# A decoder step in which value gathers, rotary key copies, gating tiles, a weight load and a square are placed anew

## The chip, the cores and the metric

The kernel runs on one core of a Trainium2 chip. The metric is the time of one execution in microseconds (us), less is better. Three timed runs of the kernel before gave 1568.81, 1569.15 and 1570.91 us, so the median is 1569.15 us.

## The reference, cut to what matters

Two layers of a hybrid decoder run for 512 prompt tokens and for 8 x 4 sample tokens (544 columns in all), in float32, with 1024 channels. Layer 0 has one input projection, a short gated convolution and a latent attention; layer 1 has a spatial gating unit. Each layer ends in a squared-ReLU MLP and a gated embedding.

```
a = rms(h);  hc, gc, gb, cq, ckv, kpe = split(a @ w_in)
kpe = rope(kpe);  q_lat = q_nope @ w_uk            # layer 0
prompt: s = q_nope.(ckv w_uk) + q_pe.kpe, causal softmax, @ (ckv w_uv)
sample: s = q_lat.past_c + q_pe.past_p over 16 pages of 128 cached rows each,
        softmax, @ past_c, then @ w_uv              # pages picked by page_table
z = gelu(a @ w_in_c);  u, v = z[:, :1024], rms(z[:, 1024:])   # layer 1
s = tril(w_s[g]) @ v[chunk, g] + b_s;  h += (u * s) @ w_out_c # g = 0..7
y = rms(h) at the very end
```

## The kernel before, in words

Activations lie with channels on the partitions, as eight chunks of 128 x 544. Weights come in 99 units of 1 MB through a ring of four slots; SyncE (SP) issues their loads in order. Each engine's list of instructions is written out by hand and the engines meet at semaphores.

The places that matter here, in order of time:

- **Start.** SP issues the loads of the gains, of the first quarter of the input, of weight unit 0, of the other three quarters, and so on. ScalarE copies each chunk times its gain into `A` (L892, semaphore `x_ready`), then squares the chunks (L896). TensorE's `in_ab(0)` and `in_ab(1)` (L480) read unit 0: 64 matmul records, chunk by chunk.
- **Key fetch.** `keys(m)` in the SP block fetches eight pages of the cached keys (144 KB each) into `kring`, whose four slots hold two such groups. From m = 2 on it waits until TensorE has scored group m - 2 (`k_scored`). `score_pair(m)` (L617) reads group m.
- **Value gathers.** POOL gathers the cached rows for the value product with indirect DMAs, four for each of 16 steps s, 1 MB a step (L423). The list `V_ORDER` gives the order 0..7, 10..13, 8, 9, 14, 15. Steps 0, 1, 6, 7, 8, 9, 14 and 15 use two buffers in the arena; the others lie in the four ring slots. Each gather of s >= 6 waits until TensorE has used an earlier buffer (`v_used`). `values_pair` (L652) reads step s.
- **Between projection and attention.** DVE ends the last convolution and the running maximum (`raw_max`, `soft_max`), copies the rotary rows of the keys from `ssum` to the eight heads of `K` (L1339, eight copies of 32 x 512), and then copies the other 64 rows of each head from PSUM (L1342, L1343), which releases the PSUM tiles `T_UK`. TensorE computes these tiles (L680) and the value tiles (L688), with the transposes of the sample probabilities (L639) between them. ScalarE exponentiates the sample scores (L914, `soft`).
- **Attention loop.** It has 32 prompt items n = 0..31 (L722 scores, L731 transposes, L743 values). `paged(n)` puts the sample work between them: `values_pair(0, n/2)` at even n below 16, `score_pair(8 + n//2)` at odd n below 16, and `values_pair(1, n - 24)` from n = 24 to 31. So key group m = 10 is needed at n = 5, 11 at 7, 12 at 9, 13 at 11, 14 at 13, 15 at 15, and step 8 + r is needed at n = 24 + r.
- **Gating.** The gMLP projection is done as groups of seven products (P1, P3, P2, P6, P5, P7, P4; L510). The dictionary `SPATIAL` says after which product of which later group a small tile is computed, all in two PSUM banks in turn: `n0` (L772) the norm of v, `t0`..`t7` (L777) transposes of one group, `T0`, `T1` (L780) transposes of the sample tokens, `M0` (L789) their mixing by 32-column matmuls, `m0`..`m7` (L784) the mixing of group g. The key ("u", j, k) stands for group j + 4 and the product k, counted 0 to 6. A tile waits until the tile two before it has been read, `M0` until `T1` has, and `m` g until `t` g has. DVE reads the tiles in the same order (L1440, L1434, L1443, L1449), but all those behind the products 0, 1 and 2 only when it has read P2, in one block (`hook(0, 1, 2)` of `combine`). POOL forms products of the gates (L450) and sums (L438 to L441).
- **End.** In `gates(1)` ScalarE takes, for each of the last eight chunks of h, first the copy times the gain (`norm_chunk`, L821) and then the square (L827), which DVE adds up (L1008) for the last norm.

## Time and profile before

| what | value |
|---|---|
| median of 3 timed runs | 1569.15 us |
| the profiled execution | 1552.78 us |
| its span, first to last instruction | 1551.0 us |
| TensorE busy | 1490.4 us, 96% |
| VectorE (DVE) busy | 1004.4 us, 65% |
| ScalarE busy | 253.8 us, 16% |
| mean granted TensorE clock | 0.981 |

The profiled execution is one run with the profiler on; it is 16.4 us shorter than the median of the timed runs. The span lies 1.8 us below its time. All stretches below are in microseconds from the start of the span. A PEclk of 1.00 is 2.4 GHz, 0.50 is 1.2 GHz. A wait row reads: who waited, for whom, total, number of times, the longest.

### The profile page before, as it was taken

The numbers are of one execution on the slowest core, as the hardware profiler recorded it, in microseconds if no ns is written. First come the engines' busy times: TensorE is split into PE (matmuls) and PEld (weight loads), VectorE is DVE, ScalarE is ACT, GpSimd is POOL, SyncE is SP. The second block draws the span as 40 slices with busy tenths as digits, with TensorE's granted clock in tenths as the row PEclk, the third lists the DMA queues.
The fourth block names the chain that finished last, engine by engine and source line by source line (L and its number), as shares of the span: only waits on it lengthen the run. The fifth ranks groups of instructions, "written<-read, shape, count | busy, mean of one in ns | idle before, by whom it ended". The sixth has DMA issues, their size and how long they took to land.

```text
span 1551.0 us, 18751 instructions
## 1 busy us (share of the span) xinstructions
PE 1490.4 (96%) x7096; PEld 1199.1 (77%) x7096; DVE 1004.4 (65%) x2020; ACT 253.8 (16%) x527; POOL 80.9 (5%) x90
## 2 busy tenths in 40 slices
PE   7999978899999999999999998999999999999995
PEld 6887734578888888888888777788888888888884
DVE  3363364868776776766755776877866767767644
ACT  4000022512101101001222320021001011011222
POOL 0012224200000000000000001300000000000000
PEclk9999998999999999999999999999999999999997
DMA  8305669422222222222213111222222222222101
GB/s 326 109 22 163 197 174 281 159 74 85 75 85 86 82 87 83 82 82 91 86 55 113 63 74 55 62 84 78 84 84 85 84 87 82 86 85 97 66 19 58
DMA packets 39323, 152.35 MB, mean 98 GB/s; under 512 B 6657, under 2 KB 19362, under 8 KB 26434
## 3 DMA queue, kind: packets, MB, share of 16 engines
q1 hardware_dynamic: 34114, 134.37, 25.0%
q0 software_dynamic: 5120, 16.78, 3.6%
q8 instruction: 57, 0.93, 0.2%
q14 instruction: 32, 0.26, 0.1%
HBM read 148.11 MB, written 3.02 MB: 97 GB/s over the span
## 4 chain that ended last, share of the span: by engine, by line
PE 92%; DVE 4%; DMA 2%; issue 1%; SPq 1%; ACT 0%; DVEq 0%
PE psum L510 66%; PE psum L480 20%; DMA arena<-in_keys 1%; PE psum L617 1%; PE psum L465 1%; PE psum L722 1%; SPq L361 1%; PE psum L743 0%; PE psum L688 0%; PE psum L602 0%; DMA ring<-in_weights 0%; PE psum L652 0%; PE psum L784 0%; DVE small L1361 0%; DVE A L1498 0%
## 5 line engine op out<-in xcount | busy, mean ns | idle before, releaser
L510 PE MATMUL psum<-arena 128*128 128x272 f32 x1920 | 457.4, 395 | 0.0
L510 PEld LDWEIGHTS psum<-arena 128*128 128x128 f32 x1920 | 366.7, 191 | 75.0
L1049 DVE TENSOR_TENSOR arena<-psum,arena 128x272 f32<-128x272 f32 x544 | 240.0, 441 | 247.6 <-PE psum L510 226.0
L480 PE MATMUL psum<-A,ring 128*128 128x272 f32 x832 | 196.8, 399 | 7.8 <-DMA ring<-in_weights 7.8
L480 PEld LDWEIGHTS psum<-A,ring 128*128 128x128 f32 x832 | 160.2, 193 | 43.2 <-DMA ring<-in_weights 7.8
L510 PE MATMUL psum<-B,ring 128*128 128x272 f32 x704 | 177.9, 396 | 4.0 <-issue 3.7
L510 PE MATMUL psum<-arena,ring 128*128 128x272 f32 x640 | 159.7, 393 | 0.0
L510 PEld LDWEIGHTS psum<-B,ring 128*128 128x128 f32 x704 | 134.1, 191 | 32.1 <-issue 4.4
L510 PE MATMUL psum<-A,ring 128*128 128x272 f32 x576 | 144.4, 393 | 1.5 <-DVE A L1423 1.5
L510 PEld LDWEIGHTS psum<-arena,ring 128*128 128x128 f32 x640 | 121.5, 190 | 24.6
L510 PEld LDWEIGHTS psum<-A,ring 128*128 128x128 f32 x576 | 109.5, 190 | 24.4 <-DVE A L1423 2.0
L844 ACT ACTIVATE arena<-psum 128x272 f32<-128x272 f32 x80 | 31.7, 396 | 541.9 <-PE psum L510 541.9
L510 PE MATMUL psum<-B,arena 128*128 128x272 f32 x352 | 88.3, 393 | 0.0
L510 PEld LDWEIGHTS psum<-B,arena 128*128 128x128 f32 x352 | 67.0, 191 | 13.6
L510 PE MATMUL psum<-A,arena 128*128 128x272 f32 x288 | 72.2, 393 | 0.0
L1029 DVE TENSOR_TENSOR arena<-ring 128x512 f32<-128x512 f32 x80 | 55.5, 694 | 13.1 <-DVE arena L1043 9.6
L1193 DVE TENSOR_TENSOR arena<-psum,rstd 128x544 f32<-128x544 f32 x18 | 12.9, 724 | 78.2 <-PE psum L480 78.0
L510 PEld LDWEIGHTS psum<-A,arena 128*128 128x128 f32 x288 | 54.8, 190 | 11.2
L1109 DVE TENSOR_TENSOR h<-h,arena 128x272 f32<-128x272 f32 x128 | 56.5, 442 | 4.4
L1108 DVE TENSOR_TENSOR arena<-arena,rstd 128x272 f32<-128x272 f32 x128 | 56.5, 441 | 4.4
L480 PE MATMUL psum<-B,ring 128*128 128x272 f32 x256 | 58.8, 393 | 0.0
L1032 DVE TENSOR_TENSOR arena<-ring 128x512 f32<-128x512 f32 x80 | 56.3, 703 | 2.8
(200 smaller groups left out, 1270.0 us busy)
## 6 DMA issues: line engine op xcount, KB each, us to landing
ring<-in_weights SPq DMA_DIRECT2D x99, 1024.0 KB, 4.8
arena<-in_keys SPq DMA_DIRECT2D x128, 144.0 KB, 5.0
arena<-in_attw SPq DMA_DIRECT2D x1, 3072.0 KB, 21.0
h<-in_xT SPq DMA_DIRECT2D x4, 544.0 KB, 7.4
out_yT<-A SPq DMA_DIRECT2D x8, 272.0 KB, 2.3
arena<-in_pemb SPq DMA_DIRECT2D x2, 544.0 KB, 5.8
arena<-in_bias SPq DMA_DIRECT2D x1, 640.0 KB, 6.3
B<-in_rope SPq DMA_DIRECT2D x1, 544.0 KB, 12.6
```

The source lines that it names most:

```text
L361: sp.dma_start(kring[:, s % 4, i % 4, :, :].rearrange("p c n -> p (c n)"), a["keys"][bass.ds(pages[i], 1), :, :].rearrange("o p n -> (o p) ...
L465: last = pe.matmul(slot(t)[:, i, 0:TH], ones[:], c[:, TH * i:TH * i + TH], start=n == 0, stop=n == len(chunks) - 1)
L480: last = pe.matmul(slot(t)[0:w.shape[-1], i, 0:TH], w, x[:, k, TH * i:TH * i + TH], start=k == 0, stop=k == ks - 1)
L510: end = pe.matmul(bank(g, n), lhs[:, c, :], x(c), start=c == 0, stop=c == 3)
L617: last = pe.matmul(psum[32 * bb:32 * bb + 32, 4, 256 * (m % 2):256 * (m % 2) + 256], qx[:, c, P * g + 32 * bb:P * g + 32 * bb + 32], kring ...
L722: pe.matmul(psum[:, n % 2, 0:(i + 1) * P], Q[0:96, hd, i * P:(i + 1) * P], K[0:96, hd, 0:(i + 1) * P], start=True, stop=True).then_inc(sc_ ...
L844: act.activation(p1_of(g), bank(g, P1), ACT.Copy).then_inc(p1_read, 1)
L1029: link(dve.tensor_tensor(wsum(g, 1), quarter(u, 1, 0), quarter(u, 1, 1), ALU.add))
L1032: dve.tensor_tensor(wsum(g, 3), quarter(u, 0, 0), quarter(u, 1, 0), ALU.subtract)
L1049: ins = dve.tensor_tensor(out, bank(g, n), more, ALU.add)
L1108: link(dve.tensor_tensor(x, x, rstd[:, half], ALU.mult))
L1109: link(dve.tensor_tensor(h[:, m, half], h[:, m, half], x, ALU.add))
```

## The change

Six edits: `V_ORDER` is dropped, so the gathers go 0 to 15; each keeps a wait on `v_used`, and steps 10 to 13 also wait until prompt items 16, 18, 20 and 22 have been scored (`sc_full` 17, 19, 21, 23). The eight copies of rotary key rows go from DVE to ScalarE, behind its fourth raw copy and ahead of its exponentials; TensorE waits for them (`k_rope`) before the first item. `SPATIAL` moves T0, t2, T1, m2, m3, t6 and t7. Weight unit 0 is loaded in two halves, the second after the second quarter of the input, and TensorE waits for each half on its own. In the last norm ScalarE squares a chunk before it copies it.

```diff
-SPATIAL = {("u", 0, 3): ["n0"], ("u", 0, 5): ["t0"], ("u", 0, 6): ["t1"],
-           ("u", 1, 0): ["T0"], ("u", 1, 1): ["t2"], ("u", 1, 2): ["T1"], ...
-           ("u", 2, 0): ["t4"], ("u", 2, 1): ["t5"], ("u", 2, 2): ["m2"], ...
+SPATIAL = {("u", 0, 3): ["n0"], ("u", 0, 4): ["T0"], ("u", 0, 5): ["t0"], ("u", 0, 6): ["t1"],
+           ("u", 1, 0): ["t2"], ("u", 1, 1): ["T1"], ("u", 1, 3): ["M0"], ...
...
-V_ORDER = [0, 1, 2, 3, 4, 5, 6, 7, 10, 11, 12, 13, 8, 9, 14, 15]
...
                 if i == 0:
-                    unit(0)
+                    sp.dma_start(ring[:, 0, 0:UNIT // 2], a["weights"][0][:, 0:UNIT // 2]).then_inc(w_first, 16)
+                elif i == 1:
+                    sp.dma_start(ring[:, 0, UNIT // 2:], a["weights"][0][:, UNIT // 2:]).then_inc(w_loaded[0], 16)
...
-            for n, s in enumerate(V_ORDER):
+            for s in range(16):
                 if 2 <= s < 6:
                     pool.wait_ge(psum_full, T_COL[2 * (s + 3) + 1] + 1)
                 elif s >= 6:
-                    pool.wait_ge(v_used, n - 5)
+                    pool.wait_ge(v_used, {6: 1, 7: 2, 8: 7, 9: 8, 14: 9, 15: 10}.get(s, s - 7))
+                if 10 <= s < 14:
+                    pool.wait_ge(sc_full, 2 * s - 3)
...
+                    if n == 0 and k == 0:
+                        pe.wait_ge(w_first, 16)
+                    elif n == 0 and k == 4 or n and n % 2 == 0 and k == 0:
+                        pe.wait_ge(w_loaded[u % SLOTS], 16 * (u // SLOTS + 1))
...
             pe.wait_ge(psum_free, T_OUTAB)
+            pe.wait_ge(k_rope, H)
...
+                if n == 6:
+                    square_chunk(n, m)
                 act.activation(X[:, m, :], h[:, m, :], ACT.Copy, scale=gain(n, m)).then_inc(x_ready, 1)
-                square_chunk(n, m)
+                if n != 6:
+                    square_chunk(n, m)
...
                 raw(0, r)
+            act.wait_ge(ql_ready, 2)
+            act.wait_ge(psum_full, T_COL[17] + 1)
+            for hd in range(H):
+                act.activation(K[64:96, hd, :], ssum[64:96, 0:TP], ACT.Copy).then_inc(k_rope, 1)
...
             soft_max(0)
-            for hd in range(H):
-                link(dve.tensor_copy(K[64:96, hd, :], ssum[64:96, 0:TP]))
```

The value gathers on POOL, from step 6 on, before:

```order
L423 DMA arena<-in_rows,vidx 128x512 [waits v_used]
L423 DMA arena<-in_rows,vidx 128x512 x3
L423 DMA arena<-in_rows,vidx 128x512 [waits v_used]
L423 DMA arena<-in_rows,vidx 128x512 x3
L423 DMA ring<-in_rows,vidx 128x512 [waits v_used]
L423 DMA ring<-in_rows,vidx 128x512 x3
```

And from step 6 on in the changed kernel:

```order
L426 DMA arena<-in_rows,vidx 128x512 [waits v_used]
L426 DMA arena<-in_rows,vidx 128x512 x3
L426 DMA arena<-in_rows,vidx 128x512 [waits v_used]
L426 DMA arena<-in_rows,vidx 128x512 x3
L426 DMA arena<-in_rows,vidx 128x512 [waits v_used]
L426 DMA arena<-in_rows,vidx 128x512 x3
L426 DMA arena<-in_rows,vidx 128x512 [waits v_used]
L426 DMA arena<-in_rows,vidx 128x512 x3
L426 DMA ring<-in_rows,vidx 128x512 [waits sc_full,v_used]
L426 DMA ring<-in_rows,vidx 128x512 x3
```

Steps 6 and 7 stay first, but the ring steps 10 to 13 now stand behind steps 8 and 9 and have a second wait.

TensorE in gating group ("u", 1, ...), from P3 to M0 (L510 is P3, P2 and P6, L777 is t2, L780 is T1, L789 is M0), before:

```order
L510 MATMUL psum<-B,arena 128x272 [waits dve_read,wsum_ready]
L510 MATMUL psum<-B,arena 128x272 x3
L777 MATMUL psum<-ident,arena 128x128 [waits psum_free]
L777 MATMUL psum<-ident,arena 128x128 x3
L510 MATMUL psum<-B,ring 128x272 [waits dve_read]
L510 MATMUL psum<-B,ring 128x272 x3
L780 MATMUL psum<-ident,arena 32x128 [waits psum_free]
L780 MATMUL psum<-ident,arena 32x128 x3
L510 MATMUL psum<-arena 128x272 [waits xt_ready,dve_read]
L510 MATMUL psum<-arena 128x272 [waits xt_ready] x3
L789 MATMUL psum<-arena 128x32 [waits psum_free]
L789 MATMUL psum<-arena 128x32 x7
```

The same products in the changed kernel (L513 is P3, P2 and P6; L790 is T1; L799 is M0):

```order
L513 MATMUL psum<-B,arena 128x272 [waits dve_read,wsum_ready]
L513 MATMUL psum<-B,arena 128x272 x3
L790 MATMUL psum<-ident,arena 32x128 [waits psum_free]
L790 MATMUL psum<-ident,arena 32x128 x3
L513 MATMUL psum<-B,ring 128x272 [waits dve_read]
L513 MATMUL psum<-B,ring 128x272 x3
L513 MATMUL psum<-arena 128x272 [waits xt_ready,dve_read]
L513 MATMUL psum<-arena 128x272 [waits xt_ready] x3
L799 MATMUL psum<-arena 128x32 [waits psum_free]
L799 MATMUL psum<-arena 128x32 x7
```

T1 now stands ahead of P2, and nothing stands between P2 and P6; M0 keeps its place behind P6.

## Rows read from the trace of the kernel before

**Rows 1.** The page, part 1: busy us, share of the span, instructions.

```profile
PE 1490.4 (96%) x7096; PEld 1199.1 (77%) x7096; DVE 1004.4 (65%) x2020; ACT 253.8 (16%) x527; POOL 80.9 (5%) x90
```

**Rows 2.** Waits of TensorE: who, for whom, total us, times, longest.

```profile
PE psum L617 <- DMA arena<-in_keys: 10.6, 4, 4.2
PE psum L480 <- DMA ring<-in_weights: 7.8, 1, 7.8
```

**Rows 3.** Timeline of the start: start us, us, instruction [idle before <-releaser].

```profile
6.59 1.39 ACT L892 ACTIVATE A<-h,gains 128x544 f32<-128x544 f32 x2
7.76 16.72 PE L480 MATMUL psum<-A,ring 128*128 128x272 f32 x64 [7.76 <-DMA ring<-in_weights]
```

**Rows 4.** Chain of waits, whole span: start us, us, what.

```profile
25.40 36.67 PE psum L480 x160
```

**Rows 5.** Timeline between projection and attention, three engines.

```profile
191.31 1.28 ACT L914 ACT_TABLE_LOAD   x1
196.92 0.72 ACT L914 ACTIVATE arena<-arena,small 128x512 f32<-128x512 f32 x1 [4.33 <-DVEq L1226]
...
196.98 3.59 DVE L1339 COPY A<-ssum 32x512 f32<-32x512 f32 x8
...
202.12 3.39 PE L680 MATMUL psum<-arena 128*128 128x512 f32 x4 [4.69 <-DVEq L1344]
...
206.07 1.88 PE L688 MATMUL psum<-arena 128*128 128x512 f32 x4
...
215.29 0.49 PE L722 MATMUL psum<-A,arena 96*128 96x128 f32 x2 [0.67 <-DVE arena L1348]
```

**Rows 6.** Timeline of TensorE in the attention loop, scores of cached keys.

```profile
217.12 1.50 PE L617 MATMUL psum<-arena 96*32 96x256 f32 x24
...
230.24 2.79 PE L617 MATMUL psum<-arena 96*32 96x256 f32 x24 [4.10 <-DMA arena<-in_keys]
...
255.63 2.79 PE L617 MATMUL psum<-arena 96*32 96x256 f32 x24 [4.19 <-DMA arena<-in_keys]
```

**Rows 7.** Stretches: length, busy us of PE, PEld, DVE, ACT, POOL, PEclk, DMA, GB/s.

```profile
219.00:270.00 51.00, 40.41 (x367) 20.29 (x366) 21.73 (x74) 15.14 (x42) 25.72 (x28) 0.83 1.03 282
...
255.60:264.00 8.40, 8.37 (x50) 3.72 (x51) 2.32 (x7) 1.65 (x4) 0.88 (x2) 0.50 1.06 301
...
272.00:293.00 21.00, 17.81 (x144) 11.48 (x139) 17.82 (x64) 13.06 (x40) 1.65 (x2) 1.00 0.13 39
```

**Rows 8.** DMA issues up to 40 us: issues, KB, median us to landing.

```profile
arena<-in_keys SPq DMA_DIRECT2D x16, 144.0 KB, 2.5
```

**Rows 9.** Timeline of POOL: first gathers of steps 10 and 14.

```profile
227.08 0.95 POOL L423 DMA_INDIRECT ring<-in_rows,vidx  x1 [0.30 <-issue]
...
293.23 0.94 POOL L423 DMA_INDIRECT arena<-in_rows,vidx  x1 [19.27 <-PE psum L652]
```

**Rows 10.** Timeline of DVE before and during the gathers of step 14.

```profile
292.85 0.43 DVE L1040 TENSOR_TENSOR arena<-B 128x272 f32<-128x272 f32 x1
...
296.52 0.44 DVE L1041 TENSOR_TENSOR arena<-B,arena 128x272 f32<-128x272 f32 x1
```

**Rows 11.** Timeline of DVE and TensorE in the gating tiles.

```profile
941.03 0.74 DVE L1440 TENSOR_SCALAR arena<-psum,arena 32x512 f32<-32x512 f32 x1
...
941.82 0.61 PE L780 MATMUL psum<-ident,arena 128*32 128x128 f32 x4 [1.99 <-DVE arena L1440]
...
944.20 1.97 PE L789 MATMUL psum<-arena 32*128 32x32 f32 x16
...
962.41 1.16 PE L784 MATMUL psum<-arena 128*128 128x128 f32 x8 [1.95 <-DVE arena L1434]
963.41 3.52 PE L510 MATMUL psum<-arena 128*128 128x272 f32 x8
```

**Rows 12.** Stretch behind 3.8 us of 32-column matmuls (L602), same columns as 7.

```profile
107.00:113.00 6.00, 6.00 (x25) 4.86 (x25) 2.39 (x9) 0.00 (x0) 1.45 (x2) 0.50 0.01 3
```

**Rows 13.** Timeline of ScalarE at the end.

```profile
1533.52 0.75 ACT L821 ACTIVATE A<-h,gains 128x544 f32<-128x544 f32 x1 [1.55 <-DVE h L1174]
```

More of the change, by code:

```diff
@@ L52 @@
 T_SP = T_N3 + 1
-SPATIAL = {("u", 0, 3): ["n0"], ("u", 0, 5): ["t0"], ("u", 0, 6): ["t1"],
[4 rows of a table removed]
+SPATIAL = {("u", 0, 3): ["n0"], ("u", 0, 4): ["T0"], ("u", 0, 5): ["t0"], ("u", 0, 6): ["t1"],
+           ("u", 1, 0): ["t2"], ("u", 1, 1): ["T1"], ("u", 1, 3): ["M0"], ("u", 1, 4): ["m0"], ("u", 1, 5): ["m1"],
+           ("u", 1, 6): ["t3"],
+           ("u", 2, 0): ["t4"], ("u", 2, 1): ["t5"], ("u", 2, 3): ["m2"], ("u", 2, 4): ["m3"], ("u", 2, 5): ["t6"],
+           ("u", 2, 6): ["t7"],
            ("u", 3, 0): ["m4"], ("u", 3, 1): ["m5"], ("u", 3, 3): ["m6"], ("u", 3, 5): ["m7"]}
@@ L251, in build @@
         x_loaded = [sem(f"x_loaded{i}") for i in range(4)]
+        w_first = sem("w_first")
         gains_loaded = sem("gains_loaded")
@@ L284, in build @@
         ql_ready = sem("ql_ready")
+        k_rope = sem("k_rope")
         qs_ready = sem("qs_ready")
@@ L572, in in_ab, with lhs @@
                 u = n // 2
-                if n % 2 == 0:
-                    pe.wait_ge(w_loaded[u % SLOTS], 16 * (u // SLOTS + 1))
                 w = ring[:, u % SLOTS, :].rearrange("p (k m) -> p k m", k=KD)
-                tile(T_COL[n], lambda k: w[:, k, (n % 2) * P:(n % 2 + 1) * P], A, KD, x_ready, 0)
+                def lhs(k):
+                    if n == 0 and k == 0:
+                        pe.wait_ge(w_first, 16)
+                    elif n == 0 and k == 4 or n and n % 2 == 0 and k == 0:
+                        pe.wait_ge(w_loaded[u % SLOTS], 16 * (u // SLOTS + 1))
+                    return w[:, k, (n % 2) * P:(n % 2 + 1) * P]
+                tile(T_COL[n], lhs, A, KD, x_ready, 0)
             in_ab(0)
```

4 rows, old and new, of the table SPATIAL are left out of this document.

## The prediction

> **What bounds the kernel now.** I read the page's busy times first: TensorE is busy for 1490.4 of 1551.0 us [rows 1], so a gain can only come from TensorE's idle time and from stretches in which it runs at half its clock. The list of TensorE's waits then says where it idles: 10.6 us for cached keys, four times, and 7.8 us for the first weights [rows 2]. The timelines place the other waits: 4.69 us for DVE ahead of the fourth key tile [rows 5], 1.99 and 1.95 us in the gating tiles [rows 11]. Last I read stretches for the granted clock and the DMA share, because after a long wait the work also costs more: the same 24 records of key scores take 1.50 us at full clock and 2.79 us behind a wait of 4.1 or 4.2 us [rows 6]. Each edit aims at one of these places, and they lie apart in time, with TensorE continuously busy between them, so the savings add.
>
> **Rotary copies to ScalarE.** DVE loses eight copies, 3.59 us [rows 5], between its maximum and its copies from PSUM. TensorE waits there: its last key tile (202.12) needs DVE's first two PSUM copies, which now start at 196.98 instead of 200.60. So it starts 3.6 us earlier, at 198.5. Its wait shrinks from 4.69 to about 1.1 us. In the row the four matmuls took 3.39 us; the same shape takes 1.88, of which some 0.15 overlaps the next, when the clock is up [rows 5], so about 1.7 us more are saved, and 0.3 on the transposes behind them, if 1.1 us of idle time leaves the clock alone. What is late next: DVE has 6.2 us of PSUM copies to do, until 203.2, then four pairs of 1.4 us for the value tiles; TensorE needs 2.2 us a pair and stays the slower one, so the first item moves from 215.29 to about 209.7. ScalarE is free at 191.31 and idle for 4.33 us before its exponential [rows 5]. A copy of 128 x 544 takes 0.70 us there [rows 3]; a 32 x 512 copy on ScalarE is not in the trace: between 0.45 (DVE's own, 3.59 / 8) and 0.70 us. I take 0.65: eight end at 196.5, the table load of 1.28 us follows, and the first exponential ends near 198.6, ahead of the transpose that needs it at 200.2. At 0.70 us it is still ahead; the cover would be gone at about 0.9. Gain 5.6 us, at least 3.6 (clock stays low) and at most 5.9.
>
> **Gathers.** From 219 to 270 us the DMA engines are full and move 282 GB/s [rows 7], that is 14.4 MB: the key groups 10 to 15 at 1.18 MB each and seven or eight value steps at 1.05 MB. Uncontended, a key fetch lands 2.5 us after its issue [rows 8], and the eight issues of a group take 4.0 us, so a group needs 6.5 us from its release. The loop gives 7.5 us for group 10 (release 218.62, when group 8 has been scored, need 230.24 - 4.10 = 226.14 [rows 6]) and about 8.5 for each later one. With the gathers beside it a group gets less than half of the bandwidth and is late. The edit takes steps 10 to 13 (4.2 MB, 14.9 us at 282 GB/s) out of this stretch into 264 to 284, where the DMA share is 0.13 [rows 7].
>
> - Group 10: its wait (4.10 us) is over at 230.24; step 10 starts only at 227.08 [rows 9], behind steps 6 and 7 in POOL's queue, which stay. I let this wait and its slow clock stand.
> - Groups 11, 12 and 13: the other 10.6 - 4.1 = 6.5 us of waits. By 235 all of groups 10, 11 and steps 6, 7 (4.5 MB) has landed, and 11 is needed at 239. Group 13 is needed at 249.1 (255.63 - 4.19 [rows 6] less the 2.3 of the two smaller waits); it is released 8.5 us before that, at 240.6, and lands by 247.5. So 6.5 us go.
> - The clock: 255.6 to 264.0 runs at 0.50 with TensorE busy for 8.37 us [rows 7]. Without the wait before it, about 4.0 us go (half of 8.37 less small waits for other engines).
> - Steps 8 and 9 now come a little earlier relative to group 15, which has 9 us for 6.5 us of transfer plus a share; I leave 0.
>
> POOL needs 5.0 us for a step (four issues 1.25 apart). From item 12 it now has eight steps in a row, 40 us, ending 19 items and 46 us later. Step 15 starts about 1.0 us later relative to its use: last issue 7.2 us ahead of need, 8.3 before. I charge 0.1 us, at most 1. Gain 10.4 us; from 2.3 (only small waits go) to 17.6 (also group 10 with its clock, 4.1 + 3.1).
>
> The trace says that gathers do not disturb DVE: a tensor_tensor of 272 columns takes 0.43 us before and 0.44 during the gathers of step 14 [rows 10], and DVE is busy for 17.8 of 21 us where they go now [rows 7]. The Trainium skill (GPSIMD Engine Reference, Specifications) says that POOL's SBUF interfaces are shared with VectorE and contend with instructions that have two SBUF inputs; by that rule these operations would be slowed; the row speaks against it for DMA issues, and the rival below on this has a small chance.
>
> The Trainium skill (DMA: Bandwidth & Descriptors, Queues, rings and completion order) says each DMA engine goes round its queues packet by packet. The trace agrees: group 10 lands 11.6 us after its release in place of 6.5. By the rule group 10, still beside steps 6 and 7, stays late, and the sum is the one below.
>
> **First unit in halves.** TensorE starts at 7.76, when 1 MB has landed; the first chunk from ScalarE is ready at 7.28 (6.59 + half of 1.39) [rows 3]. Half the weights come before that. So it starts 0.45 us earlier. The 64 records took 16.72 us; at the later pace (36.67 / 160 = 0.229 each) [rows 4] they would take 14.7, so 2 us are lost to a slow start that the edit does not touch. The later input quarters arrive as before. Gain 0.45, from 0 to 0.6.
>
> **Square ahead of its copy.** The last chunk's square waits behind its copy of 0.75 us [rows 13], of which 0.66 precedes the square's start. The chain runs square, DVE sum, ones tile, root, reciprocal, products. The copy is needed only 8 us later. Gain 0.66, from 0.6 to 0.75.
>
> **Gating tiles.** Work on TensorE is the same. Two waits change.
>
> - T1 waited 1.99 us for DVE's read of T0, which stood behind P2 [rows 11]. Now T0 is read a group earlier. But M0 stands behind P6 (1.83 us) and needs DVE to finish P2's read and scaling (1.2 us), t2 (0.95: 1.95 - 1.2 for its main part, as at t4, and some 0.2 for its sample columns) and T1 (0.74) [rows 11], so 2.9 us: a new wait of 1.06 us.
> - m2 waited 1.95 us for t4. Behind P6 that shrinks to 0.1. And P6, 3.52 us at half clock behind that wait [rows 11], gets back about 1.7, its neighbours 0.2.
> - Does the clock fall at M0? Its 1.97 us of 32-column matmuls [rows 11] now follow 1.06 us of idle time. Such thin matmuls do let it fall: behind 3.8 us of them it is 0.50 [rows 12]. A wait of 1.99 us did not; 1.95 us and then 1.16 us of 128-column matmuls did [rows 11]. That case, 3.1 us in all, is nearest to 3.0 here, so I charge 1.7 us. At the other end it is 0.
> - POOL's sums now start behind t7, one product later, and overlap two-input DVE work of the next group: 0.2 us.
>
> So 0.9 + 3.8 - 1.7 - 0.1 = 2.9 us, from 0.5 to 4.7.
>
> **Sum.** 5.6 + 10.4 + 0.45 + 0.66 + 2.9 = 20.0 us, from 1552.78 to 1532.8 for a profiled execution. The timed runs lie 16.4 us higher; I take the same difference off their median: 1569.15 - 20.0 = 1549.1 us.
>
> **Rivals.**
>
> - *Keys are late for their own sake.* With only two groups in the ring, the release and not the bandwidth would bind. For: 7.5 us against 6.5 is close, and group 10 is still late and shifts the others. Against: full DMA share throughout [rows 7]. Then a long wait and its slow clock stay, 8.2 us: 1557.3.
> - *The first wait goes too.* If steps 6 and 7 leave group 10 more room than I think, 7.2 us more: 1542.
> - *A new gating wait eats the gain.* DVE gets t2 and T1 in one block, and the clock falls for longer: 1552.
> - *POOL's issues slow DVE.* If operations with two SBUF inputs, about a quarter of DVE's 17.8 us in 272 to 293 [rows 7], doubled while POOL issues, 4.5 us would be lost: 1553.6. Rows 10 speak against it.
> - *Slower: the gathers come too late.* POOL delivers a step in 5.0 us, but items 24 to 31 use one in 2.4. If steps 10 to 15 were not ahead by item 24, they would take 6 x 5.0 + 6 us of landing against 18 us of items, 18 us more, and the clock would fall in each of six waits, about 1 us each: 1549 + 24 = 1573. It decides only when step 10 is issued 15 us later than the 264 us that I work out, which would need item 16 or step 9 to be that late. Nothing shows that.
> - *Several sizes fail at once.* The clock stays low in the rotary stretch, keys stay late, gating gives 0.5: 1562.
>
> **How the numbers follow.** Forecast 0.58, gating 0.08, slowed DVE 0.02, late keys 0.15, first wait gone 0.08, several at once 0.05, gathers late 0.04. The forecast's own range is 1546 to 1552. Late keys (1557) belong inside the 8 in 10, and half of the better case: 1543 to 1558. A measurement here can tell 0.2%, 3.1 us, from no change. Faster by more than that 0.93, within it 0.03 (several at once, with worse sizes), slower 0.04.
>
> **What would show it.** In the changed profile: TensorE's first record near 7.3; the first item near 209 to 210 and the last key tile at about 1.7 us; waits for cached keys down from 10.6 us to about 4, once, with the clock at 0.50 for one stretch of 6 us and not for the second; DMA busy between 264 and 284; no wait of TensorE on values from item 24; no wait ahead of m2's P6, one of about 1 us at M0; the last DVE sum 0.66 us nearer to the last projection record. A key wait of 4 us around group 12 or 13, or a PE wait at L652's counterpart, would prove me wrong.

## The result and the profile after

The changed kernel takes 1557.62 us (median of six runs, 1553.16 to 1559.05). The kernel before took 1568.62 us beside it (six runs). The ratio is 0.9928, 95% interval 0.9910 to 0.9946, so about 11 us are gained. The forecast was 20.0 us and 1549.1 us. The direction held and the gain is little over half of what was forecast. The time lies 0.4 us inside the wider range (1543 to 1558) and outside the forecast's own (1546 to 1552). Below, a gain against the kernel before is the ratio's share of its time. The profiled execution took 1554.70 us, with a span of 1552.7.

The page of the changed kernel, part 1, against [rows 1]: TensorE has about as much to do, and ends no earlier than in the profile of before. Part 4 of the page (the chain that ended last) names a source that the page of before does not have.

```profile
PE 1494.4 (96%) x7096; PEld 1199.0 (77%) x7096; DVE 1002.3 (65%) x2012; ACT 258.1 (17%) x535; POOL 81.6 (5%) x90
...
PE 92%; DVE 4%; another core or an unknown queue 2%; issue 1%; ACT 1%; DMA 0%; DVEq 0%; SPq 0%; ACTq 0%
```

The start and the end, TensorE, against [rows 3] and the last rows of the chain. Columns: start us, length us, instruction, and the idle time before it with what ended it.

```profile
7.36 16.79 PE L483 MATMUL psum<-A,ring 128*128 128x272 f32 x64 [7.36 <-ACT A L905]
...
1537.35 2.18 PE L468 MATMUL psum<-ssum,ones 128*128 128x272 f32 x4 [4.47 <-DVE ssum L1025]
```

TensorE now starts on ScalarE's first chunk and no longer on weights. The next group of the chain starts at 25.07 and not at 25.40 [rows 4]: 0.33 us. At the end, TensorE's ones matmuls wait 4.47 us for the last sum, where the same four waited 5.11 before: 0.64 us.

The rotary stretch (ScalarE, then TensorE), against [rows 5]:

```profile
193.78 0.60 ACT L922 ACTIVATE arena<-psum 128x512 f32<-128x512 f32 x1 [13.07 <-remote]
194.40 4.25 ACT L952 ACTIVATE A<-ssum 32x512 f32<-32x512 f32 x8
198.67 1.28 ACT L927 ACT_TABLE_LOAD   x1
```

```profile
187.51 2.80 PE L626 MATMUL psum<-arena 96*32 96x256 f32 x48
194.43 1.49 PE L635 MATMUL psum<-arena 96*128 96x32 f32 x6 [4.12 <-ACT arena L922]
195.73 8.67 PE L689 MATMUL psum<-arena 128*128 128x512 f32 x16
```

The eight copies cost ScalarE 0.53 us each, and the 4.69 us wait at the fourth key tile is gone: L689 runs its 16 matmuls in one piece. But there is a new wait of 4.12 us ahead of them. ScalarE's copy of the scores could start when L626 ended at 190.3. It starts 3.5 us later, and the profile can name no source for that ("remote": another core or an unknown queue).

Such waits return in the attention loop. Waits from 185 to 330 us, columns: who for whom, us in total, times, longest:

```profile
ACT arena L922 <- remote: 18.4, 3, 13.1
ACT arena L971 <- remote: 17.8, 6, 6.5
PE psum L741 <- DVE rbuf L1384: 15.0, 7, 3.8
DVE psum L1373 <- remote: 10.6, 5, 3.8
DVE arena L1249 <- remote: 4.0, 1, 4.0
POOL arena L426 <- remote: 1.5, 1, 1.5
```

Cached keys are no longer in this list [rows 2]. In their place TensorE waits 15.0 us for DVE, which itself stood still. One such place in the timeline:

```profile
255.21 0.66 PE L753 MATMUL psum<-arena 128*64 128x128 f32 x8
255.26 0.19 ACT L961 ACTIVATION_READ_ACCUMULATOR rbuf<-psum,small 128x1 f32 x1
255.70 0.94 POOL L426 DMA_INDIRECT arena<-in_rows,vidx  x1 [0.30 <-issue]
255.80 1.12 PE L732 MATMUL psum<-A,arena 96*128 96x512 f32 x2
256.76 0.49 PE L741 MATMUL psum<-ident,rbuf 128*128 128x128 f32 x3
256.94 0.95 POOL L426 DMA_INDIRECT arena<-in_rows,vidx  x1 [0.30 <-issue]
...
259.03 0.30 DVE L1373 TENSOR_TENSOR psum<-psum,masks 128x128 f32<-128x128 f32 x1 [3.76 <-remote]
259.08 0.49 ACT L971 ACTIVATE arena<-psum 128x384 f32<-128x384 f32 x1 [3.63 <-remote]
...
260.83 0.55 PE L741 MATMUL psum<-ident,rbuf 128*128 128x128 f32 x3 [1.52 <-DVE rbuf L1384]
```

DVE's add needs the scores of L732, ready at 256.9; ScalarE's copy needs the transposes of L741, ready at 257.3. Both start at 259.0 to 259.1, together, 1.1 us after GpSimd's fourth issue.

The trace also holds the time of every semaphore update, which these views don't print. At this place (us):

```
TensorE's work            record ends   update    later by
L626 scores, cached keys  255.28        258.87    3.59
L753 values of an item    255.87        258.96    3.09
L732 scores of an item    256.93        259.01    2.08
L661 values, cached rows  258.26        259.22    0.96
```

DVE and ScalarE start 0.02 us after the update they wait for. From 185 to 330 us, 21 of 64 updates by TensorE come more than 0.5 us after the end of the matmul record that makes them; in the profile of before all of 137 come within 0.05 us. (Counted are semaphores of which every update is on record.) So the unnamed waits are waits for TensorE whose signal is recorded late; the instructions of DVE and ScalarE are not late themselves.

The clock falls behind TensorE's own wait in several such places. Stretches (columns as in [rows 7]):

```profile
268.00:272.00 4.00, 3.66 (x23) 2.93 (x24) 2.47 (x13) 2.05 (x6) 2.26 (x3) 0.50 0.78 197
288.00:292.00 4.00, 3.42 (x21) 2.53 (x19) 2.24 (x8) 1.27 (x3) 2.28 (x3) 0.50 0.66 188
304.00:308.00 4.00, 3.54 (x22) 1.37 (x15) 2.17 (x8) 0.84 (x3) 0.32 (x1) 0.50 0.56 157
```

The gating tiles, TensorE, against [rows 11]:

```profile
944.38 0.60 PE L790 MATMUL psum<-ident,arena 128*32 128x128 f32 x4
...
949.78 1.94 PE L799 MATMUL psum<-arena 32*128 32x32 f32 x16 [1.14 <-DVE arena L1455]
951.65 2.10 PE L513 MATMUL psum<-arena 128*128 128x272 f32 x8
...
967.97 1.16 PE L794 MATMUL psum<-arena 128*128 128x128 f32 x8
968.97 2.00 PE L513 MATMUL psum<-arena 128*128 128x272 f32 x8
```

T1 (L790) and m2 (L794) no longer wait, M0 (L799) waits 1.14 us, and in this profile the product behind M0 and the one behind m2 run at full clock (2.10 and 2.00 us; behind m2 it was 3.52 before).

### The profile page after: what moved, and what is told of

The parts are those of the page before. It is cut to its first block, busy times and chain, and to the rows that moved or that the text cites. A ratio compares the mean times of both kernels' runs of the same rounds, so it can differ in the third digit from the quotient of the medians.

```text
span 1552.7 us, 18767 instructions
## 1 busy us (share of the span) xinstructions
PE 1494.4 (96%) x7096; PEld 1199.0 (77%) x7096; DVE 1002.3 (65%) x2012; ACT 258.1 (17%) x535; POOL 81.6 (5%) x90
## 3 DMA queue, kind: packets, MB, share of 16 engines
q1 hardware_dynamic: 34258, 134.37, 24.8%
## 4 chain that ended last, share of the span: by engine, by line
PE 92%; DVE 4%; another core or an unknown queue 2%; issue 1%; ACT 1%; DMA 0%; DVEq 0%; SPq 0%; ACTq 0%
PE psum L513 65%; PE psum L483 19%; PE psum L626 1%; PE psum L732 1%; PE psum L468 1%; PE psum L661 1%; PE psum L753 1%; PE psum L689 1%; DVE small L1376 1%; PE psum L697 0%; PE psum L741 0%; PE psum L611 0%; DVE rbuf L1384 0%; PE psum L794 0%
## 5 line engine op out<-in xcount | busy, mean ns | idle before, releaser
L513 PE MATMUL psum<-arena 128*128 128x272 f32 x1920 | 455.7, 393 | 0.0
L513 PEld LDWEIGHTS psum<-arena 128*128 128x128 f32 x1920 | 365.0, 190 | 75.0
L513 PE MATMUL psum<-B,ring 128*128 128x272 f32 x704 | 177.9, 395 | 4.1 <-issue 3.7
L513 PE MATMUL psum<-arena,ring 128*128 128x272 f32 x640 | 159.7, 392 | 0.0
L513 PEld LDWEIGHTS psum<-B,ring 128*128 128x128 f32 x704 | 133.9, 191 | 32.2 <-issue 4.4
L513 PE MATMUL psum<-A,ring 128*128 128x272 f32 x576 | 144.4, 393 | 1.5 <-DVE A L1438 1.5
L513 PEld LDWEIGHTS psum<-arena,ring 128*128 128x128 f32 x640 | 121.3, 190 | 24.8
L513 PEld LDWEIGHTS psum<-A,ring 128*128 128x128 f32 x576 | 109.3, 190 | 24.6 <-DVE A L1438 1.9
L513 PE MATMUL psum<-B,arena 128*128 128x272 f32 x352 | 88.3, 393 | 0.0
L513 PEld LDWEIGHTS psum<-B,arena 128*128 128x128 f32 x352 | 66.9, 191 | 13.7
L513 PE MATMUL psum<-A,arena 128*128 128x272 f32 x288 | 72.2, 392 | 0.0
L513 PEld LDWEIGHTS psum<-A,arena 128*128 128x128 f32 x288 | 54.7, 190 | 11.3
```

Of the source, the lines that this page charges most:

```text
L513: end = pe.matmul(bank(g, n), lhs[:, c, :], x(c), start=c == 0, stop=c == 3)
```

## The experiments

Each set of runs shared one chip and its own runs of the kernel before. The results give that chip the number 0 in sets 1 and 3 and 15 in set 2; whether both 0 are the same piece isn't on record. In the first set the kernel before took 1554.03 us, in the second 1566.08, in the third 1564.87, beside the changed kernel's result 1568.62. That the kernel before differs by 11 to 15 us from one to the other turned out to be half of the explanation. The table gives the stretches of the attention loop from the profile of each kernel, from the starts of items 0, 6 and 16 and of the output projection (L513's first record), in us:

```
kernel               unnamed waits   item 0-6   6-16    16-out   sum      ratio
before               no              18.71      38.49   47.38    104.58
set 1  before again  no              18.00      38.38   47.40    103.78   1.0005
       gathers only  no              19.45      29.34   50.60     99.39   0.9951
       all but them  no              19.95      37.28   46.60    103.83   0.9933
       rotary only   no              18.65      38.20   46.57    103.42   0.9959
result changed       yes             19.87      29.75   62.86    112.48   0.9928
set 2  changed again yes             20.62      31.18   61.43    113.23   0.9927
       gating only   yes             20.14      43.82   55.00    118.96   0.9976
       6, 7 later    yes             13.26      36.47   62.77    112.50   0.9926
       10 early      yes             15.67      42.06   71.53    129.26   1.0030
set 3  rows left out no              12.70      26.76   47.72     87.18   0.9781
       rows straight no              20.37      30.71   47.77     98.85   0.9850
       spread        yes             13.41      41.37   61.35    116.13   0.9970
       changed, 3rd  yes             19.70      29.68   62.61    111.99   0.9936
```

("Unnamed waits" are those after item 0. Every kernel of sets 2 and 3 has the one at 190 us.)

**The kernel before once more** (`e1_before_again`, no edit):

> The kernel before, once more, timed against itself. Theory (the profiled execution of before was an unusually fast one: 1552.78 us, while six timed ones lay at 1565 to 1571, and the profile of the changed kernel shows waits of 3 to 4 us of ScalarE and VectorE on semaphores of an unknown source that the profile of before does not have): this run's profile has a span of 1563 to 1569 us and such waits in the stretch from 180 to 320 us. Rival (the waits are a product of the changed kernel): a span of about 1551 us and no such wait. The ratio of times should be 1.000 within 0.002 either way.

1553.81 us, ratio 1.0005 (0.9981 to 1.0028), and no such wait, as the rival had it. In this set the kernel before doesn't have them. Whether the changed kernel makes them, or something that differs from set to set, stayed open here.

**The gathers alone.** The gather order and the waits of the change, nothing else:

```
-            for n, s in enumerate(V_ORDER):
+            for s in range(16):
...
-                    pool.wait_ge(v_used, n - 5)
+                    pool.wait_ge(v_used, {6: 1, 7: 2, 8: 7, 9: 8, 14: 9, 15: 10}.get(s, s - 7))
+                if 10 <= s < 14:
+                    pool.wait_ge(sc_full, 2 * s - 3)
```

> Only the gathers' new order and their waits on prompt items are put into the kernel before. If the forecast's term holds: 10.4 us faster, ratio 0.9934. If late keys are bound by their two-group ring: 2 us, 0.9985. If the unknown waits come with the gathers, wherever these are: between, 4 to 8 us, and the waits of TensorE for keys go while waits on semaphores of unknown source stand at the gathers' new places from 255 us on.

1546.96 us, ratio 0.9951 (0.9925 to 0.9976), 7.6 us less. TensorE's timeline:

```profile
232.41 2.79 PE L619 MATMUL psum<-arena 96*32 96x256 f32 x24 [4.82 <-DMA arena<-in_keys]
...
305.65 1.15 PE L654 MATMUL psum<-arena 128*32 128x256 f32 x16 [2.10 <-DMA arena<-in_rows,vidx]
```

The last gather on GpSimd, and SyncE's queue issuing the four 1 MB weight units of the output projection:

```profile
296.43 0.95 POOL L425 DMA_INDIRECT arena<-in_rows,vidx  x1 [0.30 <-issue]
```

```profile
290.81 8.77 SPq L332 DMA_DIRECT2D ring<-in_weights  x4
```

One key wait is left, that of group 10, as forecast; items 6 to 16 gain 38.38 - 29.34 = 9.0 us. The wait of group 10, 4.82 us, lies among those of the four profiles with the old order and no unnamed waits (3.37, 4.04, 4.10 and 5.30). The rows of the last step come late: 2.10 us of waiting, 3.2 us from item 16 on. In the two profiles 4.4 us remain of the gain. The timed gain, 7.6 us, has an interval of 3.7 to 11.7, so it alone doesn't exclude the 10.4 of the forecast. It fits the third expectation in size only: there is no unnamed wait.

**All but the gathers.** The changed kernel with the gathers as before:

```
+V_ORDER = [0, 1, 2, 3, 4, 5, 6, 7, 10, 11, 12, 13, 8, 9, 14, 15]
...
-            for s in range(16):
+            for n, s in enumerate(V_ORDER):
...
-                    pool.wait_ge(v_used, {6: 1, 7: 2, 8: 7, 9: 8, 14: 9, 15: 10}.get(s, s - 7))
-                if 10 <= s < 14:
-                    pool.wait_ge(sc_full, 2 * s - 3)
+                    pool.wait_ge(v_used, n - 5)
```

> The changed kernel with the gathers' old order and waits. By the forecast's terms 9.6 us faster than before, ratio 0.9939 (rotary 5.6, start 0.45, square 0.66, gating 2.9). If the rotary copies on ScalarE start late (in the changed kernel's profile they began at 194.4, not 191.3, and gained 1.4 us up to the first prompt item): 5 to 6 us, 0.9965. With e2 the two should add up to the whole change, 0.9928, if the parts are independent.

1543.63 us, ratio 0.9933 (0.9914 to 0.9952), 10.4 us less; 9.6 were expected. The gating stage, from its first tile to the products that wait for its result (997.21 us before), took 69.21 us and 69.23 in the changed kernel, against 73.43 before: 4.2 us.

**The rotary copies alone.**

```
             pe.wait_ge(psum_free, T_OUTAB)
+            pe.wait_ge(k_rope, H)
...
             for r in range(4):
                 raw(0, r)
+            act.wait_ge(ql_ready, 2)
+            act.wait_ge(psum_full, T_COL[17] + 1)
+            for hd in range(H):
+                act.activation(K[64:96, hd, :], ssum[64:96, 0:TP], ACT.Copy).then_inc(k_rope, 1)
...
-            for hd in range(H):
-                link(dve.tensor_copy(K[64:96, hd, :], ssum[64:96, 0:TP]))
```

> Only the eight rotary copies go to ScalarE. By the forecast 5.6 us faster, ratio 0.9964, with the first prompt item 5.6 us earlier. If ScalarE's fourth raw copy waits for an unknown source for 3 us there as in the changed kernel's profile: about 1.5 to 2.5 us, 0.999.

1547.18 us, ratio 0.9959 (0.9940 to 0.9979), 6.4 us less, and no unnamed wait. From the scores of the cached keys ahead of it to item 0 took 22.19 us, against 27.30 in the run of before beside it: 5.1 us. TensorE's fourth key tile, against [rows 5]:

```profile
192.53 5.40 PE L681 MATMUL psum<-arena 128*128 128x512 f32 x12
199.00 1.98 PE L681 MATMUL psum<-arena 128*128 128x512 f32 x4 [1.08 <-DVEq L1348]
```

The wait is 1.08 us (forecast 1.1), the clock stays up (1.98 us and not 3.39).

**The changed kernel again** (`e7_after_again`, no edit):

> The changed kernel once more, nothing edited. Theory (the waits of DVE and ScalarE of which the profile names no source belong to that one chip or execution, and the parts add up): no such wait here, PE waits for the keys of group 10 alone as with the gathers only (about 4.8 us), from item 16 to the output projection about 50 us and not 62.9; the gathers gained 0.9951 and everything else 0.9933, so the ratio is 0.988 to 0.990 and the time 15 to 19 us under the kernel before. Rival (the waits come of the combination of the gathers with ScalarE's copies of the rotary keys): the waits of 3 to 4 us stand again between 190 and 303 us, and the ratio stays at 0.993.

1556.58 us, ratio 0.9927 (0.9901 to 0.9954), with the unnamed waits where they were. My rival had the ratio right. Its reason fell with the next kernel.

**The gating tiles alone.**

```
-           ("u", 1, 0): ["T0"], ("u", 1, 1): ["t2"], ("u", 1, 2): ["T1"], ("u", 1, 3): ["M0"], ("u", 1, 4): ["m0"],
+           ("u", 1, 0): ["t2"], ("u", 1, 1): ["T1"], ("u", 1, 3): ["M0"], ("u", 1, 4): ["m0"], ("u", 1, 5): ["m1"],
...
```

> The kernel before with the gating tiles dealt out anew, and nothing else. The prediction: 2.9 us gained, ratio 0.9981, with 1.7 us of it lost because the clock falls again at tile M0. The theory after the profile of the changed kernel (the clock doesn't fall at M0, and the stage took 69.2 us and not 73.4): 4.2 us gained, ratio 0.9973. Nothing changes before 900 us.

1563.45 us, ratio 0.9976 (0.9959 to 0.9992), 3.8 us less. The interval (1.3 to 6.4 us) holds both expectations. At M0 this profile shows what the prediction had charged for, a fall of the clock:

```profile
955.94 1.94 PE L789 MATMUL psum<-arena 32*128 32x32 f32 x16 [1.14 <-DVE arena L1440]
957.81 3.54 PE L510 MATMUL psum<-arena 128*128 128x272 f32 x8
```

The wait and the 32-column matmuls are those of the changed kernel's profile, where the same product took 2.10 us. Of the ten profiles with the new tiles, five show the fall (from this product to the tile behind it 2.56 to 3.53 us) and five don't (1.94 us each). In three of the five, this one among them, an earlier fall behind tile `n0`, which the others have, is missing, so that the stage is no longer for it: from `n0` to the product behind `m7` it takes 61.2 to 61.5 us in eight of the ten and 63.1 to 63.2 in the two that have both falls. With the old tiles four profiles show 64.3, 65.6, 65.8 and 69.3 us.

The weightier finding is elsewhere. This kernel is the kernel before up to 900 us, and it has the unnamed waits:

```profile
194.81 0.60 ACT L909 ACTIVATE arena<-psum 128x512 f32<-128x512 f32 x1 [13.00 <-remote]
227.52 0.60 ACT L909 ACTIVATE arena<-psum 128x512 f32<-128x512 f32 x1 [2.99 <-remote]
262.86 0.60 ACT L909 ACTIVATE arena<-psum 128x512 f32<-128x512 f32 x1 [3.89 <-remote]
310.78 0.28 ACT L954 ACTIVATE arena<-psum 128x128 f32<-128x128 f32 x1 [7.80 <-remote]
```

Its loop takes 118.96 us, the same code in set 1 103.78. That is 15.2 us of longer profile beside 12.0 us by which the kernel before is slower there (1566.08 - 1554.03). So the waits come neither from the new gather order nor from ScalarE's copies. The same program has them in one set and not in another. All profiles of sets 2 and 3 have at least the one at 190 us, and none of set 1 has any; what differs between the sets, the chip or something else, is not shown, and the number 0 stands on either side.

**Steps 6 and 7 later.** The changed kernel, and

```
+                if s == 6:
+                    pool.wait_ge(sc_full, 7)
```

> The changed kernel, with the gathers of steps 6 and 7 held back until the scores of item 6 are made, so that no gather is on the queues when the keys of group 10 land. Theory (the keys of group 10 land late because two steps of gathers share the queues with them): the wait for them falls from 4.8 us to about 2 (issued from 220.3 to 226.6 and 2.5 us to land, against PE that is ready at 227.5), the half clock behind it goes too (the score group 1.5 and not 2.8 us), together 3 to 5 us less than the changed kernel, ratio 0.985 to 0.988 against before. Rival (eight page transfers, each issued 0.8 us after the last, are late by themselves): the wait stays over 4 us and the time is that of the changed kernel.

1555.51 us, ratio 0.9926 (0.9899 to 0.9954). The key wait behaves as the theory says:

```profile
225.17 1.50 PE L628 MATMUL psum<-arena 96*32 96x256 f32 x24 [0.49 <-DMA arena<-in_keys]
```

0.49 us and full clock, and items 0 to 6 take 13.26 us and not 20.6. Group 10 is late because of steps 6 and 7 alone. But items 6 to 16 take 36.47 and not 31.2, because unnamed waits moved with the gathers: DVE stands for 2.96 us until 233.38 and ScalarE for 4.48 until 234.86, where they had none, and the pair that ended at 223.65 and 228.25 is gone. The time is the same, as the rival had it, and not the 3 to 5 us less of the theory. In a set without such waits this kernel was not run.

**Step 10 early.** The changed kernel, and

```
-            for s in range(16):
+            for s in [0, 1, 2, 3, 4, 5, 6, 7, 10, 8, 9, 11, 12, 13, 14, 15]:
...
-                if 10 <= s < 14:
-                    pool.wait_ge(sc_full, 2 * s - 3)
+                if s in (7, 10):
+                    pool.wait_ge(sc_full, 7)
```

> The changed kernel, with the gathers in the order 6, 7, 10, 8, 9, 11 to 15; steps 7 and 10 wait for the scores of item 6 and none of the later ones for scores at all, so that GpSimd's queue is one step (5 us) ahead when it comes to steps 14 and 15. Theory (steps 14 and 15 are late because GpSimd still issues steps 12 and 13 when their buffers come free): the wait of about 2 us for the rows at item 31 goes, and the stretch from item 31 to the output projection is 11 us again and not 14; with half of the gain at group 10 that is 4 to 6 us less than the changed kernel, ratio 0.984 to 0.987 against before. Rival (the gathers of steps 7 and 10 now meet the keys of groups 12 and 13, issued from about 235 to 250 us): a new wait of 2 to 4 us for those keys, and the time is that of the changed kernel or 2 us over it.

1571.16 us, ratio 1.0030 (1.0013 to 1.0047), 15 us over the changed kernel. Neither expectation held. GpSimd now issues sixteen gathers one behind the other, from 264.79 to 284.49, and in the second half of them DVE and ScalarE stand still:

```profile
275.32 0.78 PE L732 MATMUL psum<-A,arena 96*128 96x128 f32 x2
276.04 0.95 POOL L426 DMA_INDIRECT ring<-in_rows,vidx  x1 [0.30 <-issue]
...
283.54 0.95 POOL L426 DMA_INDIRECT ring<-in_rows,vidx  x1 [0.30 <-issue]
286.19 0.30 DVE L1373 TENSOR_TENSOR psum<-psum,masks 128x128 f32<-128x128 f32 x1 [11.50 <-remote]
...
287.58 0.60 ACT L971 ACTIVATE arena<-psum 128x512 f32<-128x512 f32 x1 [13.61 <-remote]
```

DVE resumes 1.7 us after the last gather of the burst was issued (283.54 + 0.95). The scores that it waits for have a record that ends at 271.64; their update comes at 286.10.

**The late gathers left out.** Steps 6 to 15 stay in HBM, TensorE multiplies old rows:

```
-            for s in range(16):
+            for s in range(6):
...
-                pe.wait_ge(v_loaded[v_slot(s)], 64 * (v_use(s) + 1))
+                pe.wait_ge(v_loaded[v_slot(s)], 64)
```

> The changed kernel without the gathers of steps 6 to 15: the rows stay in HBM, and TensorE multiplies what lies in the buffers (that part of the output is left out). It prices everything the late gathers cost, keys that come late and waits without a named source alike. Theory (both come of the gathers' transfers): after 226 us no wait without a named source on DVE, ScalarE or GpSimd, no wait for keys over 1 us, and from item 0 to the output projection 93 to 97 us, against 112.5 in the changed kernel where such waits stand and about 98 where they don't. Rival (the waits without a named source belong to the program or the chip whatever is transferred): DVE stands again for 3 to 4 us at its scores near 255 us and ScalarE near 285 us, and the stretch is over 105 us.

1530.18 us, ratio 0.9781 (0.9760 to 0.9803), 25.2 us under the changed kernel. No unnamed wait after item 0, no wait for keys among TensorE's, as the theory says, and the loop takes 87.18 us; I had expected 93 to 97. Late keys, late rows and stops together cost the changed kernel 24.8 us.

**The same bytes, in a line.** Steps 6 to 15 fetch 128 rows that lie together, from the same engine at the same points of the program (other rows than the table names):

```
+                    if s >= 6:
+                        k = 128 * ((4 * s + bb) % (rows.shape[0] // 128))
+                        pool.dma_start(v_buf(v_slot(s))[:, bb, :], rows[k:k + 128, :])\
+                            .then_inc(v_loaded[v_slot(s)], 16)
+                        continue
```

> The changed kernel, in which steps 6 to 15 fetch the same amount of bytes as 128 rows in a line and not as rows picked by an index (the rows are others than the table names, so the output is others'). Theory (it is the traffic, not the kind of transfer): keys late and waits without a named source are those of the changed kernel, to 2 us in the sum. Rival (it is what GpSimd does to write the descriptors of a gather): these waits go, and the stretch from item 0 to the output projection falls to 98 us or less, as with the rows left out.

1540.92 us, ratio 0.9850 (0.9826 to 0.9874), 14.5 us under the changed kernel beside it. The theory failed. The rival had the unnamed waits right: after item 0 they are gone, and the loop takes 98.85 us where it said 98 or less. The key wait stays. TensorE's waits from 212 to 335 us:

```profile
PE psum L631 <- DMA arena<-in_keys: 7.0, 2, 5.8
PE psum L746 <- DVE rbuf L1389: 4.2, 5, 1.2
```

The queue of these transfers, from 185 to 330 us, in this kernel and then in the changed kernel's third run (packets, MB, share of 16 engines):

```profile
q0 software_dynamic: 3520, 11.54, 24.6%
```

```profile
q0 software_dynamic: 3520, 11.54, 27.9%
```

Same queue, same packets, same bytes. So the key waits need the traffic alone, and the unnamed waits need more than traffic. That it is the indirect issue is the nearest reading and not shown by itself: the rows fetched also lie elsewhere in HBM, and the issues are shorter. Without the stops the loop, 98.85 us, is close to the 99.39 of the gathers-only kernel of set 1, which has none. GpSimd's own rows in this kernel show that an indirect issue is the longer piece of work (0.94 against 0.55 us):

```profile
L431 POOL DMA_INDIRECT ring<-in_rows,vidx x16 | 15.1, 944 | 56.4 <-PE psum L488 52.8 <-issue 3.7
L428 POOL DMA_DIRECT2D arena<-in_rows x24 | 13.0, 550 | 64.8 <-PE psum L666 64.8
```

**Spread.** The gather order of "Step 10 early", with paces:

```
-                if 10 <= s < 14:
-                    pool.wait_ge(sc_full, 2 * s - 3)
+                if s in (6, 7, 10, 11, 12, 13):
+                    pool.wait_ge(sc_full, {6: 7, 7: 7, 10: 11, 11: 17, 12: 19, 13: 21}[s])
```

> The changed kernel with the gathers in the order 6, 7, 10, 8, 9, 11 to 15, where 6 and 7 wait for the scores of item 6, step 10 for those of item 10, and 11, 12, 13 for those of items 16, 18 and 20: the keys of group 10 are free of gathers as with steps 6 and 7 later, and the end of the row is a step ahead, without the eight gathers in one go that stopped DVE for 11.5 us when nothing but the buffers paced them. Theory: against the changed kernel the wait for group 10 goes (item 5 to item 6 in 3.6 us and not 9.1) and the wait for the rows of the last step too; 4 to 7 us less than the changed kernel on a chip without waits of unnamed source, 1 to 5 us less on one with them. Rival (the stops follow the gathers wherever they are put): the time is that of the changed kernel within 2 us.

1560.51 us, ratio 0.9970 (0.9958 to 0.9983), 5 us over the changed kernel; neither expectation held. The stops followed the gathers: ScalarE stood 6.07 us until 241.85 and 2.98 until 256.65, where the changed kernel has none, and items 6 to 16 took 41.37 us and not 29.68. In sets 2 and 3 no version was clearly faster than the changed kernel, short of leaving the indexed fetch out.

**The changed kernel, third time** (`e13_after_third`, no edit):

> The changed kernel a third time, nothing edited, as the measure for the three beside it. Where the kernel before takes about 1566 us, waits without a named source stand in the profile and the ratio is 0.993; where it takes about 1554 us, there are none, the parts add up and the ratio is 0.988 to 0.990.

1555.38 us, ratio 0.9936 (0.9918 to 0.9955), as in the first case of the expectation. The second case, the whole change in a set without such waits, did not come up. From its parts (0.9951 and 0.9933) it would be about 0.988, which is an estimate.

## Why the prediction was right, and where its sizes were off

The direction held, and each edit acted at the place it was meant for. The sum of 20.0 us did not hold: about 11 were measured. That the time is still inside the wider range, by 0.4 us, is partly luck. It all but equals the 1557.3 us of the rival with late keys (chance 0.15), whose reason is not what happened: waits that nobody had forecast took away nearly all of the rotary gain, and the gathers gave less than forecast for another reason. With x for a set without unnamed waits (set 1) and y for sets with them, from the profiles (one or a few each, so to a us or two):

```
term                  forecast    x      y
first unit            0.45        0.3    0.3
rotary                5.6         5.1    0.3
gathers               10.4        4.4    6.4
gating                2.9         4.2    4.2
square                0.66        0.6    0.6
sum                   20.0        14.6   11.8
timed                             ~18    11.0
```

(y for rotary: from the key scores to item 0, 26.67 us in the gating-only kernel and 26.41 in the changed one. y for the gathers: 118.96 less the mean 112.6 of three profiles of the changed kernel. The timed value of x adds the ratios of two kernels and is uncertain by some 5 us.)

**Rotary.** The mechanism was right in each step: copies off DVE, fourth key tile 3.6 us earlier, wait 4.69 to 1.08, clock kept. The copy costs 0.53 us on ScalarE, inside 0.45 to 0.70. What failed is a premise: that the wait is on the path. Where ScalarE's copy of the scores starts 3.5 us late, TensorE waits for it ahead of the key tiles, DVE has its copies done meanwhile, and in the gating-only kernel, which still has the copies on DVE, L680 runs its 16 matmuls in one piece too. The edit takes away a wait that was hidden there, and the 5.6 us become 0.3. In the measured case this is the term that is furthest off.

**Gathers.** In set 1 this is the term mis-sized most, 4.4 us in the profiles for 10.4. Of the 10.5 us, the waits and slow clock of groups 11 to 13, the runs found 9.0 (items 6 to 16). The 0.1 us charged for step 15 was 3.1 us: the last rows waited for 2.10 us and the end of the loop took 14.0 us and not 11.0. I had worked out that GpSimd's last issue would end 7.2 us ahead of need. It ended 6.2 us ahead (297.38 against 303.55), and the rows landed 8.3 us after it, beside four weight units that are issued from 290.81 on and that I had not counted on the same DMA engines. That was named in the prediction as a sign of error ("a PE wait at L652's counterpart"), and it stood there. The rest of the difference is the wait of group 10, which differs by up to 1.9 us from profile to profile with the same order. That group 10 stays late because of steps 6 and 7 was right, and holding these back removed the wait (0.49 us). The rival "keys are late for their own sake" is refuted by the same kernel, all but those 0.49 us: the group's release came at 217.27 and its landing at 225.17, 7.9 us later, where the prediction had worked out 6.5 for a group without gathers beside it.

**The waits without a name** were in neither forecast nor rivals, because the profile of before doesn't show them. They cost the kernel before 15.2 us of its loop and the changed one about 13.2 (112.6 less the 99.4 of the gathers-only kernel), so they account for the level (1554 against 1566), and for the ratio only where an edit meets them. They are also the likely source of what the prediction left as a remainder: the timed runs lay 16.4 us over the profiled execution of before. That execution has no such wait. No profile of the timed runs from 1565 to 1571 us is kept; they lie where the kernel before lies in the sets in which every profile has them. I took that offset for a constant, which it was not.

**Gating.** The waits were right: T1 none, M0 1.14 (forecast 1.06), m2 none (forecast 0.1). The 1.7 us charged for the clock at M0 were not lost in the profile of the changed kernel, where its product takes 2.10 us: 2.9 + 1.7 = 4.6 against 4.2 found. But the fall that was charged for comes in five of ten profiles with these tiles, in three of them without making the stage longer. So the reasoning on M0 was right in half of them, and neither 0 nor 1.7 us is the size of it. (The sum took 0.1 us for GpSimd's overlap, where its own line says 0.2.)

**Slowed DVE.** Not seen: DVE's add of 128x128 takes 0.30 us while a gather is being issued (at 277.40) and also where none is, at 251.77. The sentence that leaned on this row is right about the length of an instruction and missed the other kind of disturbance, a start that is late.

**First unit and square** came as forecast, 0.33 for 0.45 and 0.64 for 0.66.

## What to carry to other kernels

A gap between the profiled execution and the timed runs of the same kernel is a finding and not an offset: here the 16.4 us were most likely waits that the profile at hand did not contain, and an edit that removes a wait gains only where that wait is the last one in both kinds of execution. One profile doesn't tell whether the clock falls at a short wait either: the same wait and the same work went both ways. Before a queue is repaced, count its last element against a consumer that has already been sped up, not against the old timeline. Sixteen indexed gathers in one go went with stops of 11.5 and 13.6 us on two engines; but spreading them otherwise than the changed kernel does moved the stops and gained nothing here.

## What the runs showed of the hardware

- While indirect gathers are issued from GpSimd, TensorE's semaphore updates were recorded up to 14.5 us after the end of the matmul record that makes them (286.10 against 271.64 in "Step 10 early"). Several come out together (258.87 to 259.22 us), and DVE and ScalarE start 0.02 us after theirs. In three places they resume 1.1 to 1.7 us after the last issue of a burst (259.03, 193.78 and 286.19, after 257.89, 192.55 and 284.49). It was so in seven profiles of five kernels: 15 to 27 of 51 to 90 updates were over 0.5 us late. It came at the same instructions in those of the changed kernel (ScalarE's copy at 285.42, 289.23 and 284.87 us), and moved when the gathers were moved. With the same bytes through the same queue from rows in a line it did not happen after item 0. In that kernel the early steps are still gathered, and the wait at 190.3 to 193.8 is still there, where step 5 is issued (187.85 to 192.5).
- In set 1 the same program with the same gathers has no such wait, and none of 525 such updates in its four profiles is over 0.06 us late. Why is open. What is late is told by the updates: TensorE's signals, and not the instructions of the engines that wait. The Trainium skill (Runtime: NRT & Kernel Launch, Instruction fetch mechanics) says that an engine's instructions come in blocks by a DMA queue of its own. The trace agrees that there are such transfers: it lists two instruction queues with 14 to 15 packets from 185 to 330 us, in the before kernel of set 1 and the gating-only kernel of set 2 alike. A late block for the engine that waits would leave time between the update and its start, and there is none. Whether TensorE's matmuls themselves end late is open, as the ends of their records are modelled. So is what the recording has to do with it: in the seven profiles 50 to 81 of some 3500 semaphore updates of the program are missing from the record, in those without such waits 0 to 3.
- The same wait of 1.14 us followed by the same 1.94 us of 32-column matmuls left the clock at 1.00 in five profiles (950 to 954 us in the changed kernel's first) and was followed by 0.50 in five others (from 958.31 us on in the gating-only kernel's).
- Eight 32x512 copies take ScalarE 4.25 us, 0.53 each, beside 0.45 on DVE.
